# A Strassen-Winograd feed-forward layer: sums kept in ping-pong snapshots, reloads issued by ScalarE, three-pair blocks first

## The reference

```
xf = rms_norm(h, g_pre_ffn)
ff = silu(xf @ w_gate) * (xf @ w_up)          # 2048 -> 5632, 544 tokens
h  = h + rms_norm(ff @ w_down, g_post_ffn)    # 5632 -> 2048
```

## Time and profile before

| | us |
|---|---|
| median of 3 runs (lowest to highest) | 2483.76 (2482.35 to 2484.18) |
| the profiled execution: its time, its span | 2484.16, 2482.4 |
| PE busy, DVE busy, ACT busy | 2384.9, 1540.7, 1018.6 |
| gate and up on PE | about 973 to 1962 |
| down on PE | about 1962 to 2452 |
| final norm, transposition and stores | 2452 to 2482 |

### The profile page before, as it was taken

One profiled execution on the slowest core, in us unless ns is written; L12 is line 12 of the kernel. 1 busy time (PEld: TensorE's weight loads), 2 busy tenths in 40 slices (PEclk: granted clock), 3 DMA queues, 4 the chain that ended last, 5 costly groups with the idle time before them and its releaser, 6 DMA issues.

```text
span 2482.4 us, 42207 instructions
## 1 busy us (share of the span) xinstructions
PE 2384.9 (96%) x18280; PEld 2339.0 (94%) x18280; DVE 1540.7 (62%) x1756; ACT 1018.6 (41%) x1245; POOL 82.0 (3%) x143
## 2 busy tenths in 40 slices
PE   8999999999999995799999999999999889999998
PEld 7999999999999994799999999999999889999998
DVE  5323333343444227877777777777777678888886
ACT  6345444533333224444444444444444333333346
POOL 0000000000011110000000000000000000000002
PEclk9999999999999997899999999999999999999999
DMA  7222322232224331245444344544435756645552
GB/s 232 83 73 76 89 80 77 75 89 85 86 77 160 89 91 72 89 130 165 134 142 141 124 158 134 165 134 135 147 121 162 273 176 228 228 143 161 172 201 85
DMA packets 325916, 327.93 MB, mean 132 GB/s; under 512 B 8508, under 2 KB 282324, under 8 KB 325604
## 3 DMA queue, kind: packets, MB, share of 16 engines
q1 hardware_dynamic: 311360, 318.47, 40.0%
q10 hardware_dynamic: 14372, 6.77, 0.9%
HBM read 264.20 MB, written 61.00 MB: 131 GB/s over the span
## 4 chain that ended last, share of the span: by engine, by line
PE 80%; DVE 9%; issue 4%; ACT 4%; DMA 2%; SPq 1%; POOL 0%; DVEq 0%; ACTq 0%; POOLq 0%
PE ps L439 30%; PE ps L986 27%; PE ps L1043 17%; PE ps L753 4%; ACT t_hi L1374 2%; DVE t_lo L1768 2%; DVE panel L1782 2%; PE ps L697 1%; SPq L618 1%; DMA ff_lo_scr<-hid_lo 1%; DMA panel<-in_w_down_dram 1%; DVE xs L1790 1%; DMA misc<-in_x_sample_dram 0%; DVE misc L1794 0%; DVE wide L1758 0%
## 5 line engine op out<-in xcount | busy, mean ns | idle before, releaser
L986 PE MATMUL ps<-xs,t_hi 128*128 128x272 f32 x4928 | 941.9, 291 | 52.3 <-DVE xs L1790 20.1
L986 PEld LDWEIGHTS ps<-xs,t_hi 128*128 128x128 f32 x4928 | 779.0, 190 | 58.7 <-issue 56.3
L986 PE MATMUL ps<-xs,t_lo 128*128 128x272 f32 x2464 | 715.3, 290 | 0.0
L1768 DVE TENSOR_TENSOR t_lo<-panel,t_hi 128x1024 fp32r<-128x1024 f32 (+1 forms) x405 | 485.4, 1199 | 198.5 <-ACT t_hi L1374 190.9
L1374 ACT CAST t_hi<-panel 128x1024 fp32r<-128x1024 f32 (+1 forms) x405 | 411.8, 1022 | 464.4 <-PE ps L1043 227.1
L1043 PE MATMUL ps<-xd,t_hi 128*128 128x272 f32 x2464 | 470.9, 290 | 17.4 <-DVE t_lo L1768 8.5
L986 PEld LDWEIGHTS ps<-xs,t_lo 128*128 128x128 f32 x2464 | 466.7, 189 | 0.0
L439 PE MATMUL ps<-act_hi,w_hi 128*128 128x272 f32 (+1 forms) x2048 | 435.8, 294 | 3.5 <-DVE act_lo L1605 2.4
L439 PE MATMUL ps<-act_lo,w_hi 128*128 128x272 f32 (+1 forms) x2048 | 427.0, 290 | 0.0
L439 PE MATMUL ps<-act_hi,w_lo 128*128 128x272 f32 (+1 forms) x2048 | 427.0, 290 | 0.0
L1043 PEld LDWEIGHTS ps<-xd,t_hi 128*128 128x128 f32 x2464 | 391.1, 190 | 19.1 <-issue 10.2
(11 more groups left out here) (182 smaller groups left out, 1736.8 us busy)
## 6 DMA issues: line engine op xcount, KB each, us to landing
w_raw<-in_w_in_dram SPq DMA_DIRECT2D x96, 512.0 KB, 3.8
panel<-in_w_up_dram SPq DMA_DIRECT2D x44, 1024.0 KB, 5.7
panel<-in_w_gate_dram SPq DMA_DIRECT2D x43, 1024.0 KB, 6.8
panel<-in_w_down_dram SPq DMA_DIRECT2D x32, 1024.0 KB, 6.1
ff_hi_scr<-hid_hi SPq DMA_DIRECT2D x22, 952.0 KB, 4.5
ff_lo_scr<-hid_lo SPq DMA_DIRECT2D x22, 952.0 KB, 7.6
w_raw<-in_w_out_dram SPq DMA_DIRECT2D x32, 512.0 KB, 4.0
xd<-ff_hi_scr SPq DMA_DIRECT2D x28, 544.0 KB, 9.2
```

Source lines behind the costliest of these rows:

```text
L986: mm = nc.tensor.matmul(out, w[:, k, :], xs[:, x, part, k, :], start=begins and k == 0 and w is hi and part == 0, stop=k == KH - 1 and w i ...
L1768: V.tensor_tensor(tile_of(t_lo, i), raw_tile(i), tile_of(t_hi, i).bitcast(F32), ALU.subtract)\
```

## The change

1. `m1`, `u2` and `m7` get two buffers each; gate steps use the first, up steps the second. In an up step the sums c11, c22 and c21 are written in place over the second buffers, not to `hid`. The wait for `hid_stored` moves from c11 to `times_gate`, now the first to write `hid`. `times_gate_rest` becomes three instructions of 272 columns (before, one of 544 and one of 272), which read the buffers.
2. DVE's four hidden sums move from the gate step to the next up step, and split: two ahead of `tile_rest` of T1, two behind. ACT's `round_hidden` moves from the gate step (between the copy of m7 and the tile ahead) to the up step (between the tile of T4 and the copy of u2). DVE's `hidden_rest` moves behind c11 of that up step. In down, the last pair's sums, rounding and rest all stand in d = 1.
3. SP stores the hidden layer behind the second panel of the step, not between the two.
4. ACT issues the loads of `xd` (84 DMAs). Seven loads stand in the last up step and five in d = 1; before, twelve were issued during the last up step and d = 0.
5. `KBS` becomes [3, 3, 4, 4, 4, 4].

```
-    KBS = [4, 4, 4, 4, 3, 3]
+    KBS = [3, 3, 4, 4, 4, 4]
...
-        m1 = sb_at("m1", 134144, [P, TH])
-        u2 = sb_at("u2", 135232, [P, TH])
-        m7 = sb_at("m7", 169984, [P, TH])
-        t_hi = sb_at("t_hi", 137216, [P, RING_T, KH * P], F32R)
-        t_lo = sb_at("t_lo", 153600, [P, RING_T, KH * P], F32R)
+        m1, u2, m7 = ([sb_at(f"{name}_{odd}", (at, at_odd)[odd], [P, TH]) for odd in range(2)]
+                      for name, at, at_odd in (("m1", 134144, 171264), ("u2", 135232, 209024), ("m7", 170176, 136320)))
+        t_hi = sb_at("t_hi", 137408, [P, RING_T, KH * P], F32R)
+        t_lo = sb_at("t_lo", 153792, [P, RING_T, KH * P], F32R)
...
                 load_panel(step, 0)
-                if step >= LAST + 2:
-                    for q in range(4, 7):
-                        load_hidden_after(step - 2, q)
-                if step > 3 and step % 2 == 0 and step // 2 - 2 < FF // 2:
-                    store_hidden(step // 2 - 2)
-                if step >= LAST + 1:
-                    for q in range(2):
-                        load_hidden_after(step - 1, q)
                 if step == 1:
                     sp.wait_ge(xs_lo, 8)
                 else:
                     sp.wait_ge(tile_lo, 7 * (step - 1) + T1 + 1)
                 load_panel(step, 1)
-                if step >= LAST + 1:
-                    for q in range(2, 4):
-                        load_hidden_after(step - 1, q)
+                if step > 3 and step % 2 == 0 and step // 2 - 2 < FF // 2:
+                    store_hidden(step // 2 - 2)
...
-            def copy_out(out, step, q, letter, made, free):
+            def copy_out(out, step, q, letter, made):
                 act.wait_ge(product_done, 7 * step + q + 1)
-                if step:
-                    act.wait_ge(free, step)
-                A(out[:, :], step_bank(step, letter), ACT.Copy).then_inc(made, 1)
+
+
+                if step >= 2:
+                    if step % 2:
+                        act.wait_ge(hid_made, step // 2)
+                    else:
+                        act.wait_ge({B11: c11_made, T2: c21_made, T3: c22_made}[q], step - 1)
+                A(out[step % 2][:, :], step_bank(step, letter), ACT.Copy).then_inc(made, 1)
             def round_hidden(j):
                 act.wait_ge(hid_summed, 4 * (j + 1))
                 if j:
                     act.wait_ge(hid_stored, 32 * j)
                 nc.scalar.copy(hid_hi[:, :, :], hid[:, :, :]).then_inc(hid_rounded, 1)
...
+            def load_hidden(i):
+
+                b, q = i // 7, i % 7
+                act.wait_ge(hid_stored, 32 * first_pair[b + 1])
+                for part in range(2):
+                    act.dma_start(xd[:, i % XD, part, 0:KBS[b], :].bitcast(F32),
+                                  ff_scr[part][:, HID_OF[q], first_pair[b]:first_pair[b + 1], :])\
+                        .then_inc(xd_loaded[i % XD], 16)
+
+            def load_hidden_after(step, q):
+
+
+
+                first = []
+                if step == LAST:
+                    first = {0: (0, 1), 1: (2, 3), 2: (4, 5), 3: (6,)}.get(q, ())
+                elif step == STEPS + 1 and 0 <= q < 5:
+                    first = (7 + q,)
+                for i in first:
+                    act.wait_ge(product_done, 7 * LAST + i // 2 + 1)
+                    load_hidden(i)
+                d = step - STEPS
+                if d >= 0 and d % NQ == NQ - 1 and 0 <= q < 7:
+                    i = d // NQ * 7 + q + XD
+                    if i < 7 * len(KBS):
+                        act.wait_ge(product_done, 7 * step + q + 1)
+                        load_hidden(i)
...
-                copy_out(m1, step, B11, "a", m1_copied, c11_made)
+                copy_out(m1, step, B11, "a", m1_copied)
                 tile_high(7 * step + 4)
                 if step == 0:
                     x_high(S1, KH, 1, s_made, 1)
+                load_hidden_after(step, 0)
                 tile_high(7 * step + 5)
-                copy_out(u2, step, T2, "a", u2_copied, c21_made)
+                load_hidden_after(step, 1)
+                if not is_gate and j:
+                    round_hidden(j - 1)
+                copy_out(u2, step, T2, "a", u2_copied)
                 tile_high(7 * step + 6)
+                load_hidden_after(step, 2)
                 if step == 0:
                     act.wait_ge(tile_lo, B22 + 1)
                     x_high(S4, KH, 0, s_made, 4)
-                copy_out(m7, step, T3, "b", m7_copied, c22_made)
-                if is_gate and step:
-                    round_hidden(j - 1)
+                copy_out(m7, step, T3, "b", m7_copied)
                 tile_high(ahead)
+                load_hidden_after(step, 3)
                 tile_high(ahead + 1)
...
-                    if d == 0 and q == 6:
+                    if d == 1 and q == 4:
                         round_hidden(FF // 2 - 1)
+                    if q == 3:
+                        load_hidden_after(STEPS + d - 1, 6)
+                    else:
+                        load_hidden_after(STEPS + d, q - 4)
...
-            def quarters(step):
-                return hid if step % 2 else gate
+            def sum_of(step, up, t, n):
+
+                return up[1][:, :] if step % 2 else quarter(gate, t, n)
             def c11(step):
                 dve.wait_ge(product_done, 7 * step + B21 + 1)
                 dve.wait_ge(m1_copied, step + 1)
                 if step >= 2 and step % 2 == 0:
                     dve.wait_ge(hid_made, step // 2)
-                if step >= 3 and step % 2:
-                    dve.wait_ge(hid_stored, 32 * (step // 2))
-                V.tensor_tensor(quarter(quarters(step), 0, 0), step_bank(step, "c"), m1[:, :], ALU.add)\
+                V.tensor_tensor(sum_of(step, m1, 0, 0), step_bank(step, "c"), m1[step % 2][:, :], ALU.add)\
...
                 dve.wait_ge(silu_made, 4 * (step // 2 + 1))
-                V.tensor_tensor(quarter(hid, 0, 1), step_bank(step, "a"), quarter(gate, 0, 1), ALU.mult)                    .then_inc(c12_up, 1)
+                if step > 1:
+                    dve.wait_ge(hid_stored, 32 * (step // 2))
+                V.tensor_tensor(quarter(hid, 0, 1), step_bank(step, "a"), quarter(gate, 0, 1), ALU.mult)\
+                    .then_inc(c12_up, 1)
             def times_gate_rest(step):
                 dve.wait_ge(c21_made, step + 1)
-                V.tensor_tensor(hid[:, 0:2, :], hid[:, 0:2, :], gate[:, 0:2, :], ALU.mult)
-                V.tensor_tensor(hid[:, 3, :], hid[:, 3, :], gate[:, 3, :], ALU.mult).then_inc(hid_made, 1)
+                V.tensor_tensor(quarter(hid, 0, 0), m1[1][:, :], quarter(gate, 0, 0), ALU.mult)
+                V.tensor_tensor(quarter(hid, 1, 1), m7[1][:, :], quarter(gate, 1, 1), ALU.mult)
+                V.tensor_tensor(quarter(hid, 1, 0), u2[1][:, :], quarter(gate, 1, 0), ALU.mult).then_inc(hid_made, 1)
+
+            d21, d11, d12, d22, s1, s2, s4 = (hid[:, h, :] for h in range(7))
             def hidden_sums(j):
-                d21, d11, d12, d22, s1, s2, s4 = (hid[:, h, :] for h in range(7))
                 dve.wait_ge(hid_made, j + 1)
                 V.tensor_tensor(s1, d21, d22, ALU.add).then_inc(hid_summed, 1)
                 dve.wait_ge(hid_summed, 4 * j + 1)
                 V.tensor_tensor(d21, d11, d21, ALU.subtract).then_inc(hid_summed, 1)
+
+            def more_hidden_sums(j):
...
                 if step % 2 and step > 1:
-                    hidden_rest(step // 2 - 1)
+                    hidden_sums(step // 2 - 1)
                 tile_rest(7 * step + 4)
+                if step % 2 and step > 1:
+                    more_hidden_sums(step // 2 - 1)
                 if step == 0:
                     x_rest(S1, 7, a22)
                 if after_up:
@@ -1892,17 +1912,15 @@
                 if step == 0:
                     dve.wait_ge(s_made, 3)
                     V.tensor_tensor(a12, a12, a11, ALU.subtract).then_inc(s_made, 1)
-                elif step % 2 == 0:
+                else:
                     c11(step)
+                if step % 2 and step > 1:
+                    hidden_rest(step // 2 - 1)
                 tile_rest(7 * step + 6)
                 if step == 0:
                     x_rest(S4, 8, a12)
                     dve.wait_ge(xs_lo, 8)
                     c11(step)
-                if step % 2:
-                    c11(step)
-                if after_up:
-                    hidden_sums(step // 2 - 1)
                 tile_rest(ahead)
                 combine(step + 1, T1)
...
                 if d == 1:
-                    hidden_rest(FF // 2 - 1)
+                    hidden_sums(FF // 2 - 1)
+                    more_hidden_sums(FF // 2 - 1)
                 take_down(d, B11)
                 tile_rest(7 * step + 4)
                 if d == 0:
@@ -1955,8 +1974,8 @@
                 tile_rest(7 * step + 5)
                 take_down(d, T2)
                 tile_rest(7 * step + 6)
-                if d == 0:
```

(3 more changed lines are left out.)

23 lines of the change are left out of this document (4 added, 19 removed).

## The result

The changed kernel takes 2455.81 us (median of four runs, 2452.95 to 2458.14), beside 2483.06 us for the kernel before (2477.39 to 2484.18): a ratio of 0.989, interval 0.988 to 0.991. It is faster by 1.1%, and 17.3 us slower than forecast; the range ended at 2449.

The account below looks back on a forecast made before the run. PE, busy 96% of the span, was taken as the bound, so only its idle time could go: 49.3 us saved less 4.0 of new costs, 45.3 off 2484.16, giving 2438.9 and a median of 2438.5; range 2434 to 2449.

Parts of the forecast that it names:

- Gate and up: Gate and up steps: 21 PE stalls for c22 go, 22.9 us, and c11's wait for the store goes, 2.2.
- the moved wait: times_gate in gate steps: reached 13.6 us after the store's issue, against a landing of 7.7; costs only from 20 us.
- the store behind the second panel delays nobody else: Up steps: issuing the store behind the second panel holds up nothing else, and that panel comes earlier; no cost priced.
- The turn: From up to down: 21.4 us of stops and slower clock go, less new costs at the start of down.
- (a): Last up step: ACT's 14 DMA issues may make copies late; 0.5 us taken, bounds nothing or 8 on PE.
- R1: Rival: ScalarE's issues are slow, copies late in the last up step, 8 us for 0.5; 2446 to 2449; chance 0.17.
- (b): Start of down: pair 20's store, sharing DMA engines with reloads, lands late for times_gate; 1.0 us, bounds 0 and 3.
- (c): d = 0 and 1: DVE's extra work for the last pair makes results late for T2; 2.0 us, bounds 1 and 3.
- (d): d = 3 and 7: seven reloads and panels exceed the DMA rate in a three-pair step; 0.5 us, bounds 0 and 2.
- The end: Last steps of down: four pairs give longer products, so the remaining waits shrink; 2.1 us saved.
- The tail: Behind the last product: T4's result lies further ahead of PE's end, so the tail shortens by 0.7 us.

Follow-up runs that it names:

- e8: The changed kernel with the store of the hidden layer between the two panels of a step, as before the change: 2492.48 us, ratio 1.004.
- e7: The changed kernel with the same reloads at the same products, issued by SyncE in one queue with panels and stores: 2444.75 us, ratio 0.985.
- e3: The changed kernel with reloads 7 to 11 issued in d = 2 and not in d = 1: 2448.05 us, ratio 0.987.
- e1: The changed kernel with the old order of the blocks, KBS = [4, 4, 4, 4, 3, 3]: 2453.43 us, ratio 0.989.
- e5: The changed kernel with reloads 4 to 6 in d = 0, 7 to 11 in d = 2, later ones spread over three steps: 2438.48 us, ratio 0.982.
- e4: The changed kernel with the old block order and all reloads back on SyncE in their old places: 2449.05 us, ratio 0.988.
- e6: The changed kernel with reloads 4 to 6 in d = 0, 7 to 11 in d = 2, and the old block order: 2440.75 us, ratio 0.983.
- e10: The kernel before with only the store of a pair moved behind the second panel: 2617.30 us, ratio 1.055.
- e2: The changed kernel with reloads 4 to 6 issued in d = 0 and not in the last up step: 2448.56 us, ratio 0.988.
- e9: The kernel e5 with all reloads issued by SyncE among its panels and stores: 2434.76 us, ratio 0.981.
- e11: The kernel e5 with blocks of down in pairs 4, 3, 3, 4, 4, 4: 2433.43 us, ratio 0.981.

## Why the prediction was wrong in down and right above it

**Gate and up: right.** 22.9 + 2.2 = 25.1 forecast, 24.7 measured, and no stop left in the 43 steps behind the first. The bound of the moved wait was right too: DVE never stood for a store there, and the store landed 7.4 us after its issue. e8 adds what the prediction left unsaid: "the store behind the second panel delays nobody else" carries the whole gain of these steps.

**The turn, (a): the cover was larger than thought, and R1 was wrong.** The issues took 0.33 to 0.57 us, as priced, the longest 1.26; but they ran beside the casts and put no copy late. The price was nothing, not 0.5. What ScalarE's issuing did cost lies elsewhere, and e7 shows both parts: standing in its order it issues later than SP would (6.5 us at the second stop), and its reloads, in a queue of their own, overtake a panel in d = 7 (3.8).

**The turn, (b): the right mechanism, mis-sized, and the failed step is its upper bound.** "The store with what is ahead lands at 22 to 27", bounds 0 and 3 us. Step 43 begins 21.2 us ahead of down, at 1914.67; the store landed at 1944.6, 29.9 us from it, and PE stood 5.28 us from 1940.57, nearly the 25.6 that the working gave for the moment when T2 wants the result. Two things went wrong. The first is the rate, taken at its best, 401 GB/s, from a window of loads. From the first reload (1918.05) to the landing the DMA engines moved 9.36 MB at a mean of 353 GB/s, which is the 26.5 us that it took: 5.85 MB of reloads, 1.95 of the store, and two panels of 0.79 each, one of them issued behind the store. At 401 the same bytes would have landed 26.7 us into the step, inside the 22 to 27 (an estimate from these numbers); the rate made it 3.2 us more. Why loads and a store together get less than loads alone stays open. The second is the clock behind such a stop, which the prediction had seen in the same place of the kernel before and did not price for the new one: 2.3 of the 7.6 us (0.24 of them is in every wait).

On the order of queues the Trainium skill ("DMA: Bandwidth & Descriptors", section "Queues, rings and completion order") says that a DMA engine takes a packet from each queue in turn. The late end came, but this rule didn't decide it: in one queue (e7) the store landed at the same moment, since six of the seven reloads were issued ahead of it in the changed kernel and all seven in e7. The trace agrees with the rule in d = 7, where reloads issued behind the panel landed ahead of it from a second queue and not from the same one (the panel's 12.1 and 8.8 us). The Trainium skill's section "Issuing engines are not separate DMA queues" says that DMAs of several issuing engines run on the same 16 DMA engines, so that a second issuer saves issue time alone. The trace agrees on the rate: 353 GB/s from two queues, 346 from one in the same stretch.

**The turn, left out: the copy to `y_right`.** The prediction put the last pair's sums, rest and rounding in d = 0 and 1, and stopped there. Who waits for its store was not asked. It is `take_down` in d = 2, whose buffer lies over `hid`. In the kernel before, the store went out at 2007.68 and the copy came at 2029.37, 22 us later, unhindered. Now a step is 16 us and not 21, the rounding stands one step later, and the copy is wanted 9.6 us after the issue (1981.57 for PE, 1971.98 the issue). Alone it lands after 7.3 (e3), and with five reloads beside it after 13.6. Price 7.4 us, shown by e3.

**The turn, (c): right.** Two small stops in T2 and behind it in d = 1, 1.1 and 0.3: 1.4 for a forecast of 2.0.

**(d): the right place, mis-sized.** "They have a block of slack" was true of the reloads; it is the panel beside them that has none. Its forecast had 9 us of slack for the second panel; DVE stood for it 2.91 and 3.46 us. Forecast 0.5 with bounds 0 and 2; 9.1 measured, all of it gone without the three-pair blocks in front (e1) and nearly all removed by spreading (e5: 0.7 and 1.3). 3.8 of it goes with one queue in place of two (e7); the prediction used the rule on queues for the store alone.

**The end: right,** 2.1 forecast; no stop is left in the last steps of the changed kernel, and 2.3 us are there in each of e1, e4 and e6, which have the old order.

**The tail: 0.7 right, under a larger change of the clock.** It took 28.2 us for 30.5, 2.3 less and not 0.7. Over the runs it goes with the granted clock in it; windows of 22 us, 32 us ahead of the end, of the kernel before and then of the changed one:

```profile
2450.40:2472.40 22.00, 19.75 (x136) 19.10 (x135) 9.52 (x13) 14.30 (x24) 2.69 (x2) 0.77 0.27 97
```

```profile
2424.40:2446.40 22.00, 20.51 (x154) 19.84 (x154) 10.17 (x14) 14.30 (x24) 2.70 (x2) 0.84 0.27 98
```

At 0.77 it took 30.5 or 30.6 us (before, e1, e6), at 0.84 28.2 or 28.3 (after, e8). At the same clock the order of the blocks can be seen: at 0.92 27.4 with three pairs last (e10) and 26.6 with four (e5), at 1.00 25.8 (e4) and 25.0 or 25.1 (e2, e3, e7, e9, e11). So four pairs last are worth 0.7 to 0.8 us, as forecast, and the other 1.6 are the clock. What sets that clock stays open; it moves a run by 5 us.

**The sum, mended.** The forecast left 4.0 us lost in the new down, and 25.5 were measured, 21.5 more: 6.6 for (b), 7.4 for the copy, 8.6 for (d), less 0.6 for (c) and 0.5 for (a). With 0.4 for the forecast's other terms in down, 0.4 for gate and up, and less 3.0 for the tail and the part ahead, the profiled execution is 19.3 us over its forecast (26.0 saved and not 45.3). The median is 17.3 over, since this execution was the slowest of the four.

## What to carry to other kernels

A store that frees a buffer has a deadline: list everything that waits for it, overlaid buffers too, and compare the time from issue to that deadline with its landing under the bytes that are in flight then, neighbours behind it included. Loads with slack are best issued behind such a store and spread over the steps; here this was worth 21 of 25 us, and more than the reordering of the blocks. Where a DMA is put in a busy engine's list it starts when that list comes to it, here 11.5 us after another engine could have issued it; and where the DMA engines are full, loads in a second queue can overtake an urgent one issued before them.

## What the runs showed of the hardware

A store of 1.9 MB takes 7.4 us alone and grows with what is issued ahead of it: four reloads of three pairs 10.8, four of four pairs 13.7, seven of three pairs 16.9, seven of four pairs 21.5 (e2, e6, after, e1). ScalarE issues DMAs while its cast runs, at no cost to the cast. Behind a panel of 1 MB, without any reload, the store took 12.2 for 7.7 (e10). What is issued behind it shares the engines too: in the changed kernel the panel asked for 0.8 us behind the store had all but 0.04 of its 0.79 MB moved when the store landed. From a second queue, reloads issued behind a panel land ahead of it (after), from the same queue they don't (e7). SP's issue of a DMA mostly takes 0.3 to 0.7 us, and that of the panel right behind a store 1.4 in gate and up. At the turn, with reloads outstanding, this one took 8.29 us in the changed kernel and 3.0 to 11.2 in e1 to e9 and e11, and the store's second half 9.15 in e4; SP issued nothing else meanwhile. A stop of TensorE costs more than its length through the granted clock. Windows of the changed kernel, behind the stop of 5.28 us and behind the one of 2.35:

```profile
1946.00:1951.00 5.00, 5.00 (x24) 5.00 (x25) 3.82 (x7) 0.70 (x1) 0.00 (x0) 0.55 0.54 158
1951.00:1956.00 5.00, 5.00 (x42) 5.00 (x41) 4.11 (x7) 1.81 (x3) 0.00 (x0) 1.00 0.53 129
```

```profile
2039.00:2049.00 10.00, 10.00 (x68) 10.00 (x69) 7.44 (x10) 2.60 (x4) 0.00 (x0) 0.83 0.53 153
```

The first loses 2.1 us beyond the stop and the 0.24 of every wait, those of 2.35 and 3.23 lose 1.3 and 1.4, and the one of 0.94 none.
